# Attention stage of a decoder trunk: head weighting moved between the two halves of the key projection, softmax work put ahead of the query and key splits

## The chip, the cores and the metric

The kernel runs on one core of one Trainium2 chip. The metric is the device time of one execution in microseconds (us). A core has TensorE (PE in the rows, with its weight loads as PEld), VectorE (DVE), ScalarE (ACT), GpSimd (POOL) and SyncE (SP), which work side by side and wait for each other by semaphores. Each engine takes its own instructions in order, so an instruction that waits holds back all that stands behind it on its engine.

## What is computed

A two-layer decoder trunk on 256 tokens of width 1024, in float32: a short-convolution mixer and a convolutional feed-forward layer, then a shared key/value projection, attention with 8 heads of width 128, and a second feed-forward layer. With 256 tokens there is one block of keys, so the attention is causal softmax attention with a linear distance bias. Cut to what the change touches:

```python
k, v = jnp.split(rmsnorm(x, kv_norm) @ w_kv, 2, axis=-1)
q = (rmsnorm(x, norm_mix[1]) @ b_w_q[0]).reshape(b, s, N_HEADS, HEAD_DIM)
# for each head h and each 128 queries
s_own = einsum("bhqd,bhsd->bhqs", q_c, k_own) * scale - slopes * dist
p = softmax(where(dist >= 0, s_own, -inf))
o = einsum("bhqs,bhsd->bhqd", p, v_own)
x = x + o @ b_w_o[0]
```

## The kernel before

**Precision.** Every float32 product is made as three matmuls of rounded parts: each operand is split into a high part (a rounding copy on ScalarE) and a low part (the rest, a subtraction on VectorE). High times high, high times low and low times high are added up in PSUM. So every weight and every intermediate passes ScalarE and then VectorE before TensorE may use it.

**Weights** come in slots of 128x2048. SyncE loads them into a ring of six raw buffers; `hi(s)` (L354) rounds slot s on ScalarE, `lo(s)` (L616) subtracts on VectorE and counts `w_lo_ready`. Three places hold split slots, and a fourth (`SPARE`) a slot that is split ahead of its turn: `hi_ahead(2)` and `lo_ahead(2)` do that for the second slot of the last feed-forward layer.

**Attention** goes by pairs of heads, p = 0 to 3. Slots K and Q of pair p+1 are projected while pair p passes its softmax, so that TensorE's loop (L1207, p = 0 to 2) holds, in order: the projection of K for pair p+1 in two halves of one head each (`project(sK, 0, hA, e)`, into PSUM `pair0`), the weighting of V by the probabilities of pair p-1 (`weigh`), the scores of pair p (`scores`), the projection of Q for pair p+1 (`wide_slot`, into `pair1`), and the transposes of the probabilities of pair p (`transpose_probs`). Scores, transposed probabilities and weighted values of a head lie in one PSUM bank (`head_bank`). The banks of `acc[0]` and `acc[1]` take turns by pair, and the last pair has `pair0`.

**Helpers on the other two engines**, each once on ScalarE and once on VectorE: `kq_copy(i)` (L482) and `kq_whole(i)` (L789) add the two PSUM parts of projection i, `kq(i)` (L486, L794) splits the sum into `kq_hi` and `kq_lo`. `row_max` (L806 to L812, VectorE) adds the distance bias and finds the row maximum, `exp` (L475, ScalarE) follows, then `normal_probs` (L817, L820, VectorE). `heads_probs` (L581, L891) splits the transposed probabilities into `pt_hi` and `pt_lo`, for which `weigh` waits. `heads_mixed` (L586, L897) splits the weighted values into `mix_hi` and `mix_lo`, which the output projection reads.

**Order** is written out by hand on every engine. In the loop ScalarE and VectorE handle K of pair p+1 to its end (`kq_copy`/`kq_whole`, then `kq`), then the weighted values of pair p-1, then the softmax of pair p, then weight slot KQ0+2p+5, then Q of pair p+1, the transposed probabilities of pair p, and weight slot KQ0+2p+6.

**The tail** (L1229 to L1246): four slots of output weights, O0 to O0+3. `out_rows_of(i, t)` adds slot i for the tokens of half t into `acc[t]`. Before, the half t = 1 of O0 goes first, then the scores of heads 6 and 7, then the weighting of heads 4 and 5, then the half t = 1 of O0+1, and after that both halves t = 0.

Of the kernel before, what the change touches and what calls it, by code (L numbers as in the profile page):

```python
# [35 lines left out]
def build(nc, x, norm_mix, norm_ffn, ffn_w_up, ffn_conv, ffn_conv_b, ffn_w_down,  # L36
# [3 lines left out]
    KD = D // P  # L40
# [62 lines left out]
    with ExitStack() as ctx:  # L103
# [145 lines left out]

        def head_bank(h):  # L250

            return pair[0][:, h % 2, :] if h >= NH - 2 else acc[h // 2 % 2][h % 2][:]

        block = ctx.enter_context(nc.Block())

# [97 lines left out]
        def _(act):  # L353
            def hi(s, turn=None):  # L354

                act.wait_ge(landed[s % RAW], after(16 * (s // RAW + 1), turn, 16 * (TURN // RAW)))
                if s >= SPLIT:
                    act.wait_ge(slot_done, after(before(s) + 1, turn, TURN))
                act.activation(split_slot(s)[0], raw[:, s % RAW, :], ACT.Copy).then_inc(w_hi_ready, 2 if s + 1 in AHEAD else 1)  # L359

            def hi_ahead(o):
                s = AHEAD[o]
                act.wait_ge(landed[s % RAW], 16 * (s // RAW + 1))
                if o == 2:
                    act.wait_ge(slot_done, O0)
                act.activation(split_slot(s)[0], raw[:, s % RAW, :], ACT.Copy).then_inc(ahead_hi, 1)
# [104 lines left out]
            def exp(h):  # L471
                e = h % 2
                act.wait_ge(nbias_ready, h + 1)
                for t, cols in ((0, slice(0, 128)), (1, slice(128, 384))):
                    act.activation(logits[:, e, cols], logits[:, e, cols], ACT.Exp, bias=nbias[:, e, t:t + 1],  # L475
                                   scale=SCALE, accum_out=psums[:, e, t:t + 1]).then_inc(exp_ready, 1)

            def kq_copy(i):
                act.wait_ge(slot_done, KQ0 + i + 1)
                if i >= 2:  # L480
                    act.wait_ge(kq_lo_ready, i - 1)
                act.activation(whole[:, i % 2], cross[i % 2], ACT.Copy).then_inc(kq_cross, 1)  # L482

            def kq(i):
                act.wait_ge(kq_sum, i + 1)
                act.activation(kq_hi[:, i // 2 % 2, i % 2, :].rearrange("p (e n) -> p e n", e=2), whole[:, i % 2],  # L486
                               ACT.Copy).then_inc(kq_hi_ready, 1)
# [95 lines left out]
            def heads_mixed(p):  # L583
                for e in range(2):
                    act.wait_ge(heads_out, 2 * p + e + 1)
                    act.activation(mix_hi[:, 2 * p + e, :], head_bank(2 * p + e)[:, 0:256], ACT.Copy).then_inc(mix_hi_ready, 1)  # L586

            for p in range(NH // 2 - 1):
                kq_copy(2 * p + 2)
                kq(2 * p + 2)  # L590
                if p:
                    heads_mixed(p - 1)
                exp(2 * p)
                exp(2 * p + 1)
                hi(KQ0 + 2 * p + 5)
                kq_copy(2 * p + 3)
                kq(2 * p + 3)
                heads_probs(p)
                if p < NH // 2 - 2:
                    hi(KQ0 + 2 * p + 6)  # L600
            hi(O0 + 2)
            heads_mixed(NH // 2 - 2)
            exp(NH - 2)
            exp(NH - 1)
            hi_ahead(2)
            heads_probs(NH // 2 - 1)
            hi(O0 + 3)
            heads_mixed(NH // 2 - 1)
# [6 lines left out]
        def _(dve):  # L615
            def lo(s, turn=None):  # L616

                dve.wait_ge(w_hi_ready, after(s + 1, turn, TURN))
                whi, wlo = split_slot(s)
                dve.tensor_tensor(wlo, raw[:, s % RAW, :], whi.bitcast(F32),  # L620
                                  ALU.subtract).then_inc(w_lo_ready, 2 if s + 1 in AHEAD else 1)
# [165 lines left out]
            def kq_whole(i):  # L787
                dve.wait_ge(kq_cross, i + 1)
                dve.tensor_tensor(whole[:, i % 2], whole[:, i % 2], main[i % 2], ALU.add).then_inc(kq_sum, 1)  # L789

            def kq(i):
                dve.wait_ge(kq_hi_ready, i + 1)
                parts = [k[:, i // 2 % 2, i % 2, :].rearrange("p (e n) -> p e n", e=2) for k in (kq_hi, kq_lo)]
                dve.tensor_tensor(parts[1], whole[:, i % 2], parts[0].bitcast(F32), ALU.subtract).then_inc(kq_lo_ready, 1)  # L794
# [7 lines left out]
            def row_max(h):  # L802

                e = h % 2
                dve.wait_ge(scores_ready, h + 1)
                dve.scalar_tensor_tensor(out=logits[:, e, :], in0=dist[:], scalar=SLOPE[h] / SCALE, in1=head_bank(h)[:, 0:384],  # L806
                                         op0=ALU.mult, op1=ALU.add).then_inc(logits_ready, 1)
                dve.wait_ge(logits_ready, h + 1)
                dve.reduce_max(mx[:, e, 0:1], logits[:, e, 0:128], AX_X).then_inc(max_ready, 1)
                dve.reduce_max(mx[:, e, 1:2], logits[:, e, 128:384], AX_X).then_inc(max_ready, 1)  # L810
                dve.wait_ge(max_ready, 2 * h + 2)
                dve.tensor_scalar(nbias[:, e, :], mx[:, e, :], -SCALE, None, ALU.mult).then_inc(nbias_ready, 1)  # L812
# [81 lines left out]
            def heads_mixed(p):  # L894
                for e in range(2):
                    dve.wait_ge(mix_hi_ready, KD // 2 + 2 * p + e + 1)
                    dve.tensor_tensor(mix_lo[:, 2 * p + e, :], head_bank(2 * p + e)[:, 0:256],  # L897
                                      mix_hi[:, 2 * p + e, :].bitcast(F32), ALU.subtract).then_inc(mix_lo_ready, 1)

            for p in range(NH // 2 - 1):  # L900
                kq_whole(2 * p + 2)
                kq(2 * p + 2)
                if p:
                    heads_mixed(p - 1)
                row_max(2 * p)
                row_max(2 * p + 1)
                normal_probs(2 * p)
                normal_probs(2 * p + 1)
                lo(KQ0 + 2 * p + 5)
                kq_whole(2 * p + 3)  # L910
                kq(2 * p + 3)
                heads_probs(p)
                if p < NH // 2 - 2:
                    lo(KQ0 + 2 * p + 6)
            row_max(NH - 2)
            row_max(NH - 1)
            heads_mixed(NH // 2 - 2)
            normal_probs(NH - 2)
            normal_probs(NH - 1)
            lo(O0 + 2)  # L920
            lo_ahead(2)
            heads_probs(NH // 2 - 1)
            lo(O0 + 3)
            heads_mixed(NH // 2 - 1)
# [6 lines left out]
        def _(pe):  # L931
# [247 lines left out]
            def scores(h):  # L1179
                e, par = h % 2, h // 2 % 2  # L1180
                dst = head_bank(h)
                pe.wait_ge(kq_lo_ready, 2 * (h // 2) + 2)
                if NH - 4 <= h < NH - 2:
                    pe.wait_ge(mix_lo_ready, KD // 2 + h - 3)
                K = (kq_hi[:, par, 0, 256 * e:256 * e + 256], kq_lo[:, par, 0, 256 * e:256 * e + 256])
                Q = (kq_hi[:, par, 1, 256 * e:256 * e + 256], kq_lo[:, par, 1, 256 * e:256 * e + 256])
                split_matmul(dst[:, 0:P], ([q[:, 0:P] for q in Q], [k[:, 0:P] for k in K]), True, True)
                split_matmul(dst[:, P:3 * P], ([q[:, P:2 * P] for q in Q], K), True, True).then_inc(scores_ready, 1)
# [18 lines left out]
            for p in range(NH // 2 - 1):  # L1207
                sK, sQ = KQ0 + 2 * p + 2, KQ0 + 2 * p + 3
                wait_slot(sK)
                pe.wait_ge(kq_sum, 2 * p + 1)  # L1210
                for e in range(2):
                    last = project(sK, 0, hA, e)
                last.then_inc(slot_done, 1)
                if p:
                    weigh(2 * p - 2)
                    weigh(2 * p - 1)
                scores(2 * p)
                scores(2 * p + 1)
                pe.wait_ge(kq_sum, 2 * p + 2)
                wide_slot(sQ, 1, hB)  # L1220
                transpose_probs(2 * p)
                transpose_probs(2 * p + 1)
# [5 lines left out]

            p = NH // 2 - 1  # L1229
            wait_slot(O0)  # L1230
            pe.wait_ge(mix_lo_ready, KD // 2 + 4)
            out_rows_of(0, 1)
            scores(2 * p)
            scores(2 * p + 1)
            weigh(2 * p - 2)
            weigh(2 * p - 1)
            wait_slot(O0 + 1)
            out_rows_of(1, 1)
            pe.wait_ge(mix_lo_ready, KD // 2 + 6)
            out_rows_of(0, 0).then_inc(slot_done, 1)  # L1240
            transpose_probs(2 * p)
            transpose_probs(2 * p + 1)
            out_rows_of(1, 0).then_inc(slot_done, 1)
            weigh(2 * p)
            weigh(2 * p + 1)
            finish(O0 + 2, mix_pair(2), (mix_lo_ready, KD // 2 + 6), mix_pair(3), (mix_lo_ready, KD // 2 + 8), 4)  # L1246
# [22 lines left out]
```

## Time and profile before

| | us |
|---|---|
| runs | 599.85, 598.63, 599.07 |
| median | 599.07 |
| profiled execution, its own time | 599.85 |
| its span, first to last instruction | 598.0 |
| TensorE busy in the span | 583.9 (98%) |
| VectorE busy | 421.2 (70%) |
| ScalarE busy | 314.4 (53%) |
| mean granted TensorE clock | 0.996 |

The time of an execution is its span and some 1.9 us around it. The loop and tail of the attention stage lie between about 325 and 402 us of the span.

### The profile page before, as it was taken

What the parts mean: (1) busy time and instruction counts of PE and PEld (TensorE: products, weight loads), DVE (VectorE), ACT (ScalarE), POOL (GpSimd) and SP (SyncE); (2) the same over time, 40 slices, a digit from 0 to 9 for tenths busy, and PEclk for the clock granted to TensorE, in tenths of its full rate; (3) what the DMA queues carried; (4) which work ended last, traced back from release to release, by engine and by line L of the source; (5) the groups of instructions that cost most, each with busy time, mean ns of one, the idle gap of its engine ahead of it and who ended that gap; (6) DMA issues with size and microseconds to landing.
All of it is one profiled execution on the core that took longest, in us unless ns stands there. A gap on an engine that the chain in (4) does not pass through costs nothing.

```text
span 598.0 us, 8163 instructions
## 1 busy us (share of the span) xinstructions
PE 583.9 (98%) x3119; PEld 498.6 (83%) x3119; DVE 421.2 (70%) x508; ACT 314.4 (53%) x380; POOL 10.1 (2%) x22
## 2 busy tenths in 40 slices
PE   8999999999999999999999989899999999999995
PEld 6988888888888888888878878788888888888884
DVE  4688876678666666668786778787686666666764
ACT  5543563566545445546445655645674545544541
POOL 2000000000000000000100000000000000000000
PEclk9999999999999999999999999899999999999999
DMA  8995658354566556555565344263556655654001
GB/s 282 344 296 200 216 184 276 122 200 162 192 211 211 179 173 210 192 166 196 181 210 178 144 140 142 71 219 122 204 193 212 209 168 186 210 180 170 0 0 71
DMA packets 80911, 107.99 MB, mean 181 GB/s; under 512 B 1833, under 2 KB 71665, under 8 KB 80882
## 3 DMA queue, kind: packets, MB, share of 16 engines
q1 hardware_dynamic: 80160, 104.97, 53.1%
q10 hardware_dynamic: 722, 2.63, 1.3%
q8 instruction: 19, 0.31, 0.2%
q14 instruction: 10, 0.08, 0.0%
HBM read 106.54 MB, written 1.05 MB: 180 GB/s over the span
## 4 chain that ended last, share of the span: by engine, by line
PE 90%; DVE 5%; ACT 3%; issue 1%; POOL 0%; ACTq 0%; DVEq 0%; POOLq 0%
PE pair L951 33%; PE pair L952 17%; PE acc L993 8%; PE acc L995 8%; PE acc L997 8%; PE pair L935 3%; PE pair L937 3%; PE pair L936 3%; DVE wgt L620 2%; ACT wgt L359 2%; PE pair L1007 2%; PE acc L937 1%; PE acc L936 1%; PE acc L935 1%; PE acc L1116 1%
## 5 line engine op out<-in xcount | busy, mean ns | idle before, releaser
L951 PE MATMUL pair<-hA,wgt 128*128 128x512 f32 x864 | 304.7, 397 | 0.0
L620 DVE TENSOR_TENSOR wgt<-raw,wgt 128x2048 fp32r<-128x2048 f32 x94 | 214.9, 2291 | 62.3 <-ACT wgt L359 62.3
L952 PE MATMUL pair<-hA,wgt 128*128 128x256 f32 x864 | 241.4, 279 | 0.0
L951 PEld LDWEIGHTS pair<-hA,wgt 128*128 128x128 f32 x864 | 162.2, 188 | 38.7
L359 ACT ACTIVATE wgt<-raw 128x2048 fp32r<-128x2048 f32 x94 | 179.4, 1912 | 26.3 <-PE acc L997 22.8
L952 PEld LDWEIGHTS pair<-hA,wgt 128*128 128x128 f32 x864 | 162.8, 188 | 0.6
L993 PE MATMUL acc<-wgt,kq_hi 128*128 128x512 f32 x160 | 49.8, 392 | 0.0
L995 PE MATMUL acc<-wgt,kq_hi 128*128 128x512 f32 x160 | 49.7, 392 | 0.0
L997 PE MATMUL acc<-wgt,kq_lo 128*128 128x512 f32 x160 | 49.3, 389 | 0.0
L426 ACT ACTIVATE scratch<-scratch 128x512 f32<-128x512 f32 x22 | 13.9, 632 | 59.7 <-DVE scratch L698 59.7
L440 ACT ACTIVATE scratch<-pair 128x512 f32<-128x512 f32 x20 | 11.9, 595 | 59.9 <-PE pair L952 59.9
L719 DVE TENSOR_TENSOR scratch<-scratch,pair 128x512 f32<-128x512 f32 x20 | 13.7, 686 | 32.6 <-ACT scratch L440 32.6
L995 PEld LDWEIGHTS acc<-wgt,kq_hi 128*128 128x128 f32 x160 | 30.0, 188 | 6.8
L935 PE MATMUL pair<-wgt,hA 128*128 128x512 f32 (+1 forms) x96 | 34.7, 362 | 1.0 <-DVE v_lo L799 1.0
L997 PEld LDWEIGHTS acc<-wgt,kq_lo 128*128 128x128 f32 x160 | 30.0, 188 | 6.7
L937 PE MATMUL pair<-wgt,hA 128*128 128x512 f32 (+1 forms) x96 | 34.1, 355 | 0.0
L936 PE MATMUL pair<-wgt,hA 128*128 128x512 f32 (+1 forms) x96 | 34.0, 354 | 0.0
L993 PEld LDWEIGHTS acc<-wgt,kq_hi 128*128 128x128 f32 x160 | 28.8, 188 | 5.7
L698 DVE SCALAR_TENSOR_TENSOR scratch<-scratch,f_par 128x255 f32<-128x255 f32 (+1 forms) x80 | 33.2, 477 | 0.0
L723 DVE TENSOR_TENSOR scratch<-scratch,pair 128x512 f32<-128x512 f32 x20 | 13.8, 688 | 23.7 <-ACT scratch L447 23.7
L377 ACT ACTIVATE acc<-xs 128x512 f32<-128x512 f32 x20 | 12.0, 602 | 27.3 <-DVE xs L631 24.0
L418 ACT ACTIVATE scratch<-scratch,f_par 128x256 f32<-128x256 f32 x40 | 21.6, 590 | 1.5 <-DVE scratch L719 1.5
(143 smaller groups left out, 610.0 us busy)
## 6 DMA issues: line engine op xcount, KB each, us to landing
raw<-in_ffn_w_up SPq DMA_DIRECT2D x44, 1024.0 KB, 5.1
raw<-in_ffn_w_down SPq DMA_DIRECT2D x22, 1024.0 KB, 4.8
raw<-in_a_w_in SPq DMA_DIRECT2D x11, 1024.0 KB, 11.5
raw<-in_w_kv SPq DMA_DIRECT2D x8, 1024.0 KB, 5.2
raw<-in_a_w_out SPq DMA_DIRECT2D x4, 1024.0 KB, 4.9
raw<-in_b_w_q SPq DMA_DIRECT2D x4, 1024.0 KB, 5.6
raw<-in_b_w_o SPq DMA_DIRECT2D x4, 1024.0 KB, 5.3
raw<-in_a_w_in SPq DMA_DIRECT2D x2, 512.0 KB, 7.1
```

Of the source, the lines that this page charges most:

```text
L359: act.activation(split_slot(s)[0], raw[:, s % RAW, :], ACT.Copy).then_inc(w_hi_ready, 2 if s + 1 in AHEAD else 1)
L418: ins = act.activation(g[:, e, :], gate[:, e, :], ACT.Identity, bias=f_par[:, l, bass.ds(f + TAPS * FT, 1)], scale=f_par[:, l, bass.ds(f + ...
L620: dve.tensor_tensor(wlo, raw[:, s % RAW, :], whi.bitcast(F32), ALU.subtract).then_inc(w_lo_ready, 2 if s + 1 in AHEAD else 1)
L698: dve.scalar_tensor_tensor(out=dst, in0=gate[:, e, 0:S - back], scalar=f_par[:, l, bass.ds(f + (TAPS - 1 - back) * FT, 1)], in1=dst, op0=A ...
L935: pe.matmul(dst, sh, mh, start=first, stop=False)
L936: pe.matmul(dst, sh, ml, start=False, stop=False)
L937: return pe.matmul(dst, sl, mh, start=False, stop=last)
L951: pe.matmul(dst.rearrange("p (a n) -> p a n", a=2), whi[:, w], hid[:, :, k, :], start=k == 0, stop=False)
L952: last = pe.matmul(dst[:, 0:S], wlo[:, w], hid[:, 0, k, :], start=False, stop=k == KD - 1)
L993: pe.matmul(acc[t][h][:], ah, wh[h], start=first, stop=False)
L995: pe.matmul(acc[t][h][:], ah, wl[h], start=False, stop=False)
L997: last = pe.matmul(acc[t][h][:], al, wh[h], start=False, stop=False)
```

## The change

**PSUM banks.** `head_bank` gives `acc[1]` to all heads below 6; the pairs no longer take turns. In return every `scores(h)` with h of 2 or more waits for `mix_lo` of head h-2, the last reader of what lay in the bank.

**Loop on TensorE.** The two `weigh` calls move from behind both halves of the K projection to a place between them.

**Loop on ScalarE and VectorE.** `heads_mixed(p-1)` moves ahead of `kq_copy`/`kq_whole(2p+2)`, and `kq(2p+2)` moves from directly behind it to behind the softmax and weight slot KQ0+2p+5.

**Tail.** The half t = 0 of O0 and O0+1 goes first (it reads `mix_lo` of fewer heads and writes the free `acc[0]`), `weigh` of heads 4 and 5 stands ahead of the scores of heads 6 and 7, and `hi_ahead(2)`/`lo_ahead(2)` stand ahead of `heads_mixed(2)`, with slot O0+2 split later in exchange. On VectorE `heads_mixed(2)` comes ahead of the row maxima of heads 6 and 7.

The diff of the loop and the tail on TensorE and of the loop on VectorE (ScalarE's is the same in kind):

```diff
-            return pair[0][:, h % 2, :] if h >= NH - 2 else acc[h // 2 % 2][h % 2][:]
+            return pair[0][:, h % 2, :] if h >= NH - 2 else acc[1][h % 2][:]
...
             for p in range(NH // 2 - 1):
-                kq_whole(2 * p + 2)
-                kq(2 * p + 2)
                 if p:
                     heads_mixed(p - 1)
+                kq_whole(2 * p + 2)
                 row_max(2 * p)
                 row_max(2 * p + 1)
                 normal_probs(2 * p)
                 normal_probs(2 * p + 1)
                 lo(KQ0 + 2 * p + 5)
+                kq(2 * p + 2)
                 kq_whole(2 * p + 3)
                 kq(2 * p + 3)
                 heads_probs(p)
...
+            lo_ahead(2)
+            heads_mixed(NH // 2 - 2)
             row_max(NH - 2)
             row_max(NH - 1)
-            heads_mixed(NH // 2 - 2)
             normal_probs(NH - 2)
             normal_probs(NH - 1)
             lo(O0 + 2)
-            lo_ahead(2)
...
-                if NH - 4 <= h < NH - 2:
-                    pe.wait_ge(mix_lo_ready, KD // 2 + h - 3)
+                if h >= 2:
+                    pe.wait_ge(mix_lo_ready, KD // 2 + h - 1)
...
-                for e in range(2):
-                    last = project(sK, 0, hA, e)
-                last.then_inc(slot_done, 1)
+                project(sK, 0, hA, 0)
                 if p:
                     weigh(2 * p - 2)
                     weigh(2 * p - 1)
+                project(sK, 0, hA, 1).then_inc(slot_done, 1)
...
-            pe.wait_ge(mix_lo_ready, KD // 2 + 4)
-            out_rows_of(0, 1)
+            pe.wait_ge(mix_lo_ready, KD // 2 + 2)
+            out_rows_of(0, 0)
+            weigh(2 * p - 2)
+            weigh(2 * p - 1)
             scores(2 * p)
             scores(2 * p + 1)
-            weigh(2 * p - 2)
-            weigh(2 * p - 1)
             wait_slot(O0 + 1)
-            out_rows_of(1, 1)
+            pe.wait_ge(mix_lo_ready, KD // 2 + 4)
+            out_rows_of(1, 0)
             pe.wait_ge(mix_lo_ready, KD // 2 + 6)
-            out_rows_of(0, 0).then_inc(slot_done, 1)
+            out_rows_of(0, 1).then_inc(slot_done, 1)
             transpose_probs(2 * p)
             transpose_probs(2 * p + 1)
-            out_rows_of(1, 0).then_inc(slot_done, 1)
+            out_rows_of(1, 1).then_inc(slot_done, 1)
```

What stands where, first on VectorE in the loop at p = 1, before. `wgt<-raw` is a weight slot's `lo`, `scratch<-scratch,pair` is `kq_whole`, `kq_lo` is `kq`, `pt_lo` is `heads_probs`, `mix_lo` is `heads_mixed`, and `scratch<-dist,acc` opens `row_max`:

```order
L620 TENSOR_TENSOR wgt<-raw,wgt 128x2048 [waits w_hi_ready]
L789 TENSOR_TENSOR scratch<-scratch,pair1 128x512 [waits kq_cross]
L794 TENSOR_TENSOR kq_lo<-scratch,kq_hi 128x512 [waits kq_hi_ready]
L891 TENSOR_TENSOR pt_lo<-acc00,pt_hi 128x384 [waits pt_hi_ready]
L891 TENSOR_TENSOR pt_lo<-acc01,pt_hi 128x384 [waits pt_hi_ready]
L620 TENSOR_TENSOR wgt<-raw,wgt 128x2048 [waits w_hi_ready]
L789 TENSOR_TENSOR scratch<-scratch,pair0 128x512 [waits kq_cross]
L794 TENSOR_TENSOR kq_lo<-scratch,kq_hi 128x512 [waits kq_hi_ready]
L897 TENSOR_TENSOR mix_lo<-acc00,mix_hi 128x256 [waits mix_hi_ready]
L897 TENSOR_TENSOR mix_lo<-acc01,mix_hi 128x256 [waits mix_hi_ready]
L806 SCALAR_TENSOR_TENSOR scratch<-dist,acc10 128x384 [waits scores_ready]
```

The same stretch of VectorE in the changed kernel:

```order
L620 TENSOR_TENSOR wgt<-raw,wgt 128x2048 [waits w_hi_ready]
L794 TENSOR_TENSOR kq_lo<-scratch,kq_hi 128x512 [waits kq_hi_ready]
L789 TENSOR_TENSOR scratch<-scratch,pair1 128x512 [waits kq_cross]
L794 TENSOR_TENSOR kq_lo<-scratch,kq_hi 128x512 [waits kq_hi_ready]
L891 TENSOR_TENSOR pt_lo<-acc10,pt_hi 128x384 [waits pt_hi_ready]
L891 TENSOR_TENSOR pt_lo<-acc11,pt_hi 128x384 [waits pt_hi_ready]
L620 TENSOR_TENSOR wgt<-raw,wgt 128x2048 [waits w_hi_ready]
L897 TENSOR_TENSOR mix_lo<-acc10,mix_hi 128x256 [waits mix_hi_ready]
L897 TENSOR_TENSOR mix_lo<-acc11,mix_hi 128x256 [waits mix_hi_ready]
L789 TENSOR_TENSOR scratch<-scratch,pair0 128x512 [waits kq_cross]
L806 SCALAR_TENSOR_TENSOR scratch<-dist,acc10 128x384 [waits scores_ready]
```

The K split has left the place between `kq_whole` and the row maximum, and stands between the weight slot and Q's `kq_whole`, so ahead of `pt_lo`.

TensorE in the tail, around heads 4 to 7, in the changed kernel (`acc10<-pt_hi,v_hi` is `weigh`, `pair0<-kq_hi` is `scores`, `wgt,mix_hi` is an output slot):

```order
L997 MATMUL acc01<-wgt,mix_lo 128x512
L935 MATMUL acc10<-pt_hi,v_hi 128x256 [waits pt_lo_ready]
...
L937 MATMUL acc11<-pt_hi,v_lo 128x128
L935 MATMUL pair0<-kq_hi 128x128 [waits mix_lo_ready,kq_lo_ready]
...
L937 MATMUL pair0<-kq_hi,kq_lo 128x256
L993 MATMUL acc00<-wgt,mix_hi 128x512 [waits mix_lo_ready,w_lo_ready]
```

Before, the scores stood ahead of the weighting here and waited for `kq_lo_ready` alone; now they stand behind it and wait for `mix_lo` of the values that it makes.

## Rows read from the trace of the kernel before

**Rows 1.** The page: the chain that ended last, by engine.

```profile
PE 90%; DVE 5%; ACT 3%; issue 1%; POOL 0%; ACTq 0%; DVEq 0%; POOLq 0%
```

**Rows 2.** Waits between 325 and 402 us: waiter, releaser, us in total, times, longest.

```profile
ACT kq_hi L486 <- DVE scratch L789: 13.9, 7, 2.5
DVE wgt L620 <- ACT wgt L359: 8.4, 9, 1.1
...
PE acc L1194 <- DVE scratch L820: 3.2, 4, 1.0
...
PE pair L935 <- DVE kq_lo L794: 2.0, 1, 2.0
```

**Rows 3.** Timeline of PE in the loop: start us, us, instruction, idle before and releaser.

```profile
333.75 0.22 PE L935 MATMUL acc<-kq_hi 128*128 128x128 f32 x1
...
341.43 0.47 PE L951 MATMUL pair<-hA,wgt 128*128 128x512 f32 x1
...
344.29 0.39 PE L951 MATMUL pair<-hA,wgt 128*128 128x512 f32 x1
...
347.06 0.28 PE L935 MATMUL acc<-pt_hi,v_hi 128*128 128x256 f32 x1
...
348.38 0.28 PE L935 MATMUL acc<-kq_hi 128*128 128x128 f32 x1
...
349.82 0.40 PE L951 MATMUL pair<-wgt 128*128 128x512 f32 x1
...
356.54 0.55 PE L1194 MATMUL acc<-ident,scratch 128*128 128x128 f32 x3 [1.01 <-DVE scratch L820]
...
358.00 0.47 PE L951 MATMUL pair<-hA,wgt 128*128 128x512 f32 x1
```

**Rows 4.** Timeline of PE in the tail.

```profile
374.56 0.70 PE L993 MATMUL acc<-wgt,mix_hi 128*128 128x512 f32 x2
...
379.58 0.33 PE L935 MATMUL pair<-kq_hi 128*128 128x128 f32 x1 [2.04 <-DVE kq_lo L794]
...
381.06 0.33 PE L935 MATMUL acc<-pt_hi,v_hi 128*128 128x256 f32 x1
...
383.43 1.16 PE L993 MATMUL acc<-wgt,mix_hi 128*128 128x512 f32 x2
```

**Rows 5.** Timeline of DVE in the loop and the tail.

```profile
334.57 0.69 DVE L789 TENSOR_TENSOR scratch<-scratch,pair 128x512 f32<-128x512 f32 x1
335.96 0.69 DVE L794 TENSOR_TENSOR kq_lo<-scratch,kq_hi 128x512 fp32r<-128x512 f32 x1 [0.70 <-ACT kq_hi L486]
336.57 0.55 DVE L806 SCALAR_TENSOR_TENSOR scratch<-dist,acc 128x384 f32<-128x384 f32 x1
...
342.12 2.29 DVE L620 TENSOR_TENSOR wgt<-raw,wgt 128x2048 fp32r<-128x2048 f32 x1 [1.05 <-ACT wgt L359]
344.33 0.68 DVE L789 TENSOR_TENSOR scratch<-scratch,pair 128x512 f32<-128x512 f32 x1
...
346.32 1.01 DVE L891 TENSOR_TENSOR pt_lo<-acc,pt_hi 128x384 fp32r<-128x384 f32 x2
...
384.08 0.42 DVE L897 TENSOR_TENSOR mix_lo<-acc,mix_hi 128x256 fp32r<-128x256 f32 x1 [0.46 <-ACT mix_hi L586]
```

**Rows 6.** Timeline of ACT in the loop and the tail.

```profile
333.94 0.60 ACT L482 ACTIVATE scratch<-pair 128x512 f32<-128x512 f32 x1 [1.75 <-PE pair L952]
...
340.20 1.90 ACT L359 ACTIVATE wgt<-raw 128x2048 fp32r<-128x2048 f32 x1
...
346.33 1.91 ACT L359 ACTIVATE wgt<-raw 128x2048 fp32r<-128x2048 f32 x1
```

**Rows 7.** Stretches: bounds, length, each engine's busy us (count), granted clock, DMA.

```profile
372.00:374.00 2.00, 0.64 (x4) 0.31 (x3) 1.49 (x8) 1.68 (x7) 0.00 (x0) 1.00 0.00 0
...
382.00:383.00 1.00, 1.00 (x7) 1.00 (x6) 0.97 (x3) 0.38 (x1) 0.00 (x0) 0.50 0.03 9
...
385.00:386.00 1.00, 1.00 (x6) 0.83 (x5) 0.83 (x4) 1.00 (x5) 0.00 (x0) 1.00 0.00 0
```

More of the change, by code:

```diff
@@ L588, in _ @@
             for p in range(NH // 2 - 1):
-                kq_copy(2 * p + 2)
-                kq(2 * p + 2)
                 if p:
                     heads_mixed(p - 1)
+                kq_copy(2 * p + 2)
                 exp(2 * p)
@@ L600, in _ @@
                     hi(KQ0 + 2 * p + 6)
-            hi(O0 + 2)
+            hi_ahead(2)
             heads_mixed(NH // 2 - 2)
@@ L604, in _ @@
             exp(NH - 1)
-            hi_ahead(2)
+            hi(O0 + 2)
             heads_probs(NH // 2 - 1)
@@ L900, in _ @@
             for p in range(NH // 2 - 1):
-                kq_whole(2 * p + 2)
-                kq(2 * p + 2)
                 if p:
                     heads_mixed(p - 1)
+                kq_whole(2 * p + 2)
                 row_max(2 * p)
@@ L909, in _ @@
                 lo(KQ0 + 2 * p + 5)
+                kq(2 * p + 2)
                 kq_whole(2 * p + 3)
```

## The prediction

> **What bounds the kernel now.** I read the chain that ended last first: 90% of it is TensorE [rows 1], so time can only be won or lost where TensorE stands idle or runs slowly. The list of waits then says where that is. In the attention stage TensorE waits four times for the probabilities, 3.2 us in all, and once 2.0 us for `kq_lo` of the last pair [rows 2]. The order behind 402 us is the same in both kernels, and with the chain on TensorE I take it that what such a wait gains or loses moves the end by as much.
>
> The timelines show why it waits. One turn of the loop takes 16.57 us (341.43 to 358.00), of which TensorE's own work is less: K projection 5.63 (341.43 to 347.06), `weigh` 1.32, `scores` 1.44 (to 349.82), Q projection as long as K without its restart, 5.56, and two sets of transposes, 0.75; together 14.7. So 1.87 us of each turn are a stall, seen in front of the transposes [rows 3]. The other side is a ring of ScalarE and VectorE: VectorE waits for each weight slot's high part (8.4 us in nine waits) and ScalarE for each `kq_whole` (13.9 us in seven) [rows 2]. The two alternate and set the turn; TensorE trails.
>
> In the tail TensorE starts the last scores at 379.58 after 2.04 us idle, and then runs slowly: the two `weigh` take 2.37 us (381.06 to 383.43) in place of 1.32, and the first pair of output matmuls 1.16 in place of 0.70 [rows 3, 4]. The granted clock there is 0.50, which is 1.2 GHz, and it is 1.00 (2.4 GHz) again from 385 on. Before it fell, TensorE had been idle for 2.04 us. The shorter stalls in the loop (1.01 us and one more just behind it, with TensorE busy for 0.64 of 2 us) left it at 1.00 [rows 7]. I count the slow stretch at 1.05 + 0.46, about 1.5 us.
>
> **The change part by part.** I carry three dates through the loop, on the clock of the trace of before; until 334 us nothing differs.
>
> *K's split leaves the place ahead of the row maximum.* `kq_whole(2)` starts at 334.57 and now the row maximum follows it after 0.61 us (the spacing of such an operation, 335.96 to 336.57), at 335.18 and not 336.57: 1.39 us earlier [rows 5]. The scores are there by then (they start at 333.75 and take 1.44, head by head) [rows 3]. This carries on through the exponentials to `hi(KQ0+5)`, 340.20 before and 338.81 now [rows 6], and its `lo`, 342.12 before and 340.73 now [rows 5].
>
> *It comes back ahead of Q's.* Behind `lo` stands now `kq_lo` of K, 0.61 us, and only then Q's `kq_whole`, on which `pt_lo` hangs. Of 1.39 us won 0.78 is left for `pt_lo`: it starts at 345.54 and not 346.32, and its first head is ready 0.55 later, at 346.09 [rows 5].
>
> *`weigh` moves ahead of the second half of K.* This is the term on which all hangs. Before, TensorE came to `weigh` at 347.06, after 5.63 us of K, and `pt_lo` was just there. Now it comes after half of K, at 344.29, and finds `pt_lo` missing until 346.14: a stall of 1.85 us [rows 3]. The stall in front of the transposes goes, since the softmax is done 1.4 us earlier and TensorE comes later. One stall takes the place of the other.
>
> *The ring is now closed through TensorE.* `kq_copy` of K needs both halves of K, and the second now stands behind `weigh`, so also behind `pt_lo`. One turn of the new ring, each step from rows: `weigh` 1.32 and second half 2.77 (344.29 to 347.06) [rows 3]; from K's end to ScalarE's copy 0.20 (333.75 to 333.94) [rows 3, 6]; copy 0.63 (to 334.57); `kq_whole` 0.61; row maximum to `hi` 3.63 (336.57 to 340.20); `hi` to `lo` 1.92; `lo` 2.21 (342.12 to 344.33); `kq_lo` 0.61; `kq_whole` to `pt_lo` 1.99 (344.33 to 346.32); `pt_lo` of the first head 0.55 and 0.05 to TensorE [rows 5, 6]. The sum is 16.49 us, against 16.57 before. The loop wins 0.1 us a turn and no more. `weigh` of heads 4 and 5 starts at 346.14 + 2 x 16.49 = 379.12.
>
> *The new wait of the scores for `mix_lo`, in the loop.* It waits behind the whole second half of K. `mix_lo` of both heads follows `lo(KQ0+6)`, which starts at 345.54 + 0.01 + 1.92 = 347.47 and frees VectorE at 349.68; the first head is ready 0.42 later at 350.10. TensorE wants it at 346.14 + 1.32 + 2.77 = 350.23. I take nothing for it. Its cover is 0.13 us; behind the scores stand the Q projection and the transposes, so what is late here is paid in full.
>
> *The tail.* Behind `pt_hi` of heads 4 and 5 ScalarE does `hi_ahead(2)` first: `pt_lo` starts at 378.52, `hi_ahead` at 378.53 as `hi` did beside it before (346.32 and 346.33) [rows 5, 6], `lo_ahead` 1.92 later at 380.45, then 2.21 of VectorE to 382.66, and only then `mix_lo`, 0.42 for head 4 [rows 5], with 0.05 at 383.13. The scores of heads 6 and 7 wait for that. TensorE has ended `weigh` at 379.12 + 1.32 = 380.44 and stands for 2.7 us. Scores end at 383.13 + 1.44 = 384.57. Before, the same point (slot O0+1 begins) was at 383.43, or at 382.38 without the slow clock [rows 4]. The change **loses 2.2 us** here. Behind it no new wait: by the same steps the last probabilities are ready at about 388.5 and wanted at 390.1, `pt_lo` of head 6 at 392.3 and wanted at 393.6, `mix_lo` of head 7 at 396.4 and wanted at 397.7, so 1.2 us of cover at the least. Using one bank pair for all heads, the other order of the output halves, and the later `hi`/`lo` of O0+2 cost nothing beyond these waits.
>
> *The clock.* Before had one long stall (2.04 us) and one slow stretch (1.5 us). The changed kernel has five: 1.85 at p = 1, 16.49 - 14.7 = 1.8 at p = 2, and in the tail 1.8, then 1.3 us of work, then 2.7. Bounds for the two in the loop: nothing each, as after the stalls of 1.0 us, or 1.5 each, as after that of 2.04. They are nearer to the second, but a little shorter; I take one of the two. For the tail pair I take one slow stretch as before, between 1.0 (partly under the 2.7 us wait) and 3 (it reaches into the output slots).
>
> By the Trainium skill ("TensorE: Matmul & The Clock Gate", section "Why this matters for your kernels") the clock is lost in idle gaps longer than any single one here. The trace of before disagrees, since its 2.04 us sufficed; by that rule the sum would lack every slow stretch and be 600.5, the second case below.
>
> **Sum.** Profiled execution 599.85 + 2.2 + 1.5 = 603.6. The median lies 0.8 below the profiled execution, perhaps for want of the slow stretch, so the forecast is **602.8**, 0.6% above 599.07.
>
> **The rivals.**
>
> *The clock stays up.* All of the above holds but no stall brings the clock down: 599.85 - 1.5 + 2.2 = 600.5. For it: stalls of 1.85 and less are not 2.04. Against it: two of them, 1.8 and 2.7, lie within 6 us. 0.12.
>
> *Trade one for one.* The loop is even as computed and the tail's wait is short, because `mix_lo` comes early, where `lo_ahead` is done by the time `weigh` ends. That needs 2.2 us less than the rows give: 599.1. 0.06.
>
> *The stalls go (faster).* If `pt_lo` were ready when TensorE comes to `weigh`, at 344.3, the ring would be short, and TensorE's 14.7 us would be the turn: 2 x 1.87 won in the loop, 2.0 for `kq_lo` of the last pair and 1.5 of slow clock, 7.3 in all, 591.8. It decides at 1.8 us: so much earlier must `pt_lo` be. Against it stand four rows in series (`lo` 2.21, `kq_lo` 0.61, `kq_whole` to `pt_lo` 1.99). 0.05.
>
> *The scores' wait bites in the loop too.* If heads' splitting is over 0.13 us later than I count, each turn pays the rest, and a slow stretch may follow at both loop stalls: with two more slow stretches and 0.5 us a turn, 599.1 + 2.2 + 3 + 1 = 605.3 and more. 0.05.
>
> **How the numbers follow.** Forecast 0.72, its own range from 601.3 (no slow stretch in the loop) to 604.6 (two). The range to hold eight in ten starts at the second case, 600.5, and ends at 605.2. A measurement of this kernel can tell about 0.2% (1.2 us) from no change. Slower by over that: 0.72 + 0.09 + 0.05 = 0.86; the second case lies just at this bound, and gives 0.03 to "same", which with the trade is 0.09; faster is 0.05.
>
> **What would show it.** In the changed kernel's list of waits `weigh` (PE L935) must wait for `pt_lo` L891 three times, for 1.8 us each, the scores in the tail once for `mix_lo` L897 for 2.7, and the transposes hardly at all; a turn of the loop must be 16.5 us; stretches at clock 0.50 must follow the stalls. It is wrong if the transposes still wait, if a turn is near 14.7, or if the scores at p = 1 wait for `mix_lo`.

## The result and the profile after

The changed kernel is slower: 605.35 us median (603.85 to 606.12) against 599.46 us for the kernel before beside it, a ratio of 1.0096 with a 95% interval of 1.0076 to 1.0115. In a second comparison it took 604.19 us (603.67 to 606.1) against 600.1, a ratio of 1.0077 (1.0061 to 1.0093). The forecast of 602.8 had the direction right and the size too small: +3.7 us was forecast, and +5.9 and +4.1 were measured. The first median, of four runs, lies 0.15 us above the range. The record of the first comparison has fifteen executions of the changed kernel, from 603.57 to 606.82 us with a median of 605.17, so the true middle lies close to the range's upper end.

The waits of TensorE's instructions between 325 and 408 us of the changed kernel (waiter, releaser, us in total, times, longest), to be held against [rows 2]:

```profile
PE acc L935 <- DVE pt_lo L891: 5.5, 3, 1.9
...
PE pair L935 <- DVE mix_lo L897: 2.5, 1, 2.5
```

The 3.2 us in front of the transposes (L1194) and the 2.0 us for `kq_lo` are gone. In their place `weigh` (acc L935) waits three times for `pt_lo`, and the scores of heads 6 and 7 (pair L935) once for `mix_lo`. Here are the places in time (start us, us, instruction, idle before it and its releaser), beside [rows 3, 4]:

```profile
333.14 0.22 PE L935 MATMUL acc<-kq_hi 128*128 128x128 f32 x1
...
345.54 0.39 PE L935 MATMUL acc<-pt_hi,v_hi 128*128 128x256 f32 x1 [1.82 <-DVE pt_lo L891]
...
351.38 0.22 PE L935 MATMUL acc<-kq_hi 128*128 128x128 f32 x1
...
363.79 0.39 PE L935 MATMUL acc<-pt_hi,v_hi 128*128 128x256 f32 x1 [1.83 <-DVE pt_lo L891]
...
368.05 0.22 PE L935 MATMUL acc<-kq_hi 128*128 128x128 f32 x1
...
380.45 0.39 PE L935 MATMUL acc<-pt_hi,v_hi 128*128 128x256 f32 x1 [1.87 <-DVE pt_lo L891]
...
384.57 0.44 PE L935 MATMUL pair<-kq_hi 128*128 128x128 f32 x1 [2.53 <-DVE mix_lo L897]
...
387.27 1.05 PE L993 MATMUL acc<-wgt,mix_hi 128*128 128x512 f32 x2
...
394.32 0.82 PE L1194 MATMUL pair<-ident,scratch 128*128 128x128 f32 x6
```

The second turn, from `weigh` to `weigh`, is 16.66 us (363.79 to 380.45). The first is 18.25 us (345.54 to 363.79), and the clock tells why. These are stretches of the changed kernel (bounds, length, each engine's busy us, granted clock, DMA), beside [rows 7]:

```profile
346.00:348.00 2.00, 2.00 (x12) 2.00 (x11) 1.12 (x1) 1.31 (x3) 0.00 (x0) 0.56 0.31 127
348.00:350.00 2.00, 2.00 (x9) 1.66 (x9) 1.84 (x3) 0.20 (x1) 0.00 (x0) 0.58 0.00 0
...
364.00:366.00 2.00, 2.00 (x17) 1.91 (x17) 1.06 (x2) 1.76 (x3) 0.00 (x0) 1.00 0.52 178
382.00:384.00 2.00, 0.04 (x1) 0.00 (x0) 2.00 (x1) 0.42 (x2) 0.00 (x0) 0.95 0.00 0
384.00:386.00 2.00, 1.43 (x7) 1.46 (x8) 0.76 (x3) 0.00 (x0) 0.00 (x0) 0.50 0.00 0
...
388.00:390.00 2.00, 2.00 (x6) 1.52 (x6) 1.49 (x8) 1.68 (x9) 0.00 (x0) 0.50 0.00 0
390.00:392.00 2.00, 2.00 (x9) 1.62 (x8) 0.91 (x4) 1.76 (x1) 0.00 (x0) 0.84 0.03 8
```

A mean clock of 0.56 over 2 us says that TensorE spent 1.76 us of them at 0.50, which is 1.2 GHz. So it ran slowly for 3.4 us between 346 and 350, behind the first stall. It did so again for 6.8 us, from just ahead of 384 until inside 390 to 392, behind the stalls of 1.87 and 2.53 us. In the kernel before, the one slow stretch lasted 3.4 us (381.2 to 384.6). Behind the stall at p = 2, which was as long as that at p = 1, the clock stayed at 1.00.

What the low clock cost can be read off the start times. The measure is the same piece of work at full clock: for `weigh` to the scores that of p = 2 above, and for the tail these rows of the changed kernel with its stalls filled (first experiment below):

```profile
384.07 0.30 PE L935 MATMUL pair<-kq_hi 128*128 128x128 f32 x1 [1.35 <-DVE mix_lo L897]
...
385.53 0.63 PE L993 MATMUL acc<-wgt,mix_hi 128*128 128x512 f32 x2
...
390.99 0.82 PE L1194 MATMUL pair<-ident,scratch 128*128 128x128 f32 x6
```

From `weigh` to the scores TensorE took 5.84 us at p = 1 (345.54 to 351.38) and 4.26 at p = 2 (363.79 to 368.05): 1.6 us. The last scores took 2.70 us (384.57 to 387.27) in place of 1.46: 1.2 us. The two half slots of output weights after them took 7.05 us (387.27 to 394.32) in place of 5.46: 1.6 us. Together the slow clock cost 4.4 us in this execution. In the profiled execution of before it cost 1.6: 1.05 on `weigh`, and 0.6 on the half slots, which took 6.08 (383.43 to the transposes at 389.51) and 5.5 in the kernel before with its stall filled.

The mean clock is 1.00 from 0 to 325 us and from 402 to 584 us in each of the ten profiles, so a slow clock in another stage plays no part.

### The profile page after: what moved, and what is told of

Same layout as the page of the kernel before. It is cut to its first block, busy times and chain, and to the rows that moved or that the text cites. A ratio compares the mean times of both kernels' runs of the same rounds, so it can differ in the third digit from the quotient of the medians.

```text
span 602.9 us, 8168 instructions
## 1 busy us (share of the span) xinstructions
PE 585.9 (97%) x3119; PEld 501.0 (83%) x3119; DVE 421.4 (70%) x508; ACT 314.7 (52%) x380; POOL 10.1 (2%) x22
## 3 DMA queue, kind: packets, MB, share of 16 engines
HBM read 106.54 MB, written 1.05 MB: 178 GB/s over the span
## 4 chain that ended last, share of the span: by engine, by line
PE 91%; DVE 5%; ACT 3%; issue 1%; POOL 0%; DVEq 0%; ACTq 0%; POOLq 0%
PE pair L951 34%; PE pair L952 17%; PE acc L993 8%; PE acc L995 8%; PE acc L997 8%; PE pair L935 3%; PE pair L937 3%; PE pair L936 3%; PE pair L1007 2%; DVE wgt L620 2%; PE acc L935 1%; PE acc L937 1%; PE acc L936 1%; ACT wgt L359 1%; PE acc L1116 1%
## 5 line engine op out<-in xcount | busy, mean ns | idle before, releaser
L935 PE MATMUL pair<-wgt,hA 128*128 128x512 f32 (+1 forms) x96 | 34.7, 362 | 1.0 <-DVE v_lo L799 1.0
```

The costliest lines, as they stand in the source:

```text
L935: pe.matmul(dst, sh, mh, start=first, stop=False)
```

## The experiments

Theory A says that the loss is the stalls' (about 2.2 us) and that all the rest is the clock that falls behind them. Its rivals: the rest is something else (B), one part of the change gives back what it wins (C), or the place of `weigh` alone costs the time and the single bank pair nothing (D).

### All stalls filled

```diff
                 project(sK, 0, hA, 0)
                 if p:
+                    fill(acc[0][1][:, 0:P], 4)
                     weigh(2 * p - 2)
...
             out_rows_of(0, 0)
+            pe.wait_ge(kq_sum, NH - 1)
+            fill(pair[0][:, 0, 0:P], 4)
             weigh(2 * p - 2)
             weigh(2 * p - 1)
+            fill(pair[0][:, 0, 0:P], 5)
             scores(2 * p)
```

`fill(bank, n)` issues n matmuls of the identity into a bank that is free then; the trace shows two matmul records for each call.

> The changed kernel, with matmuls of the identity (results unused) put into its stalls: 4 calls ahead of the weighting at p = 1 and 2, 4 ahead of that in the tail, 5 ahead of the scores of heads 6 and 7. They keep TensorE busy while it waits and should not move a wait's end. Theory A (the waits cost 2.2 us, all the rest of the loss is the clock that falls after them): no stretch below clock 1.00 between 325 and 402 us, and 599.5 - 1.0 (the clock's share in the kernel before) + 2.2 = 600.7, between 600.0 and 601.4. Theory B (the rest is something else, late work on the other engines or a transfer): about as the changed kernel, 604.5 to 605.5.

Measured: 601.36 us median, and twelve runs lie between 601.0 and 601.73. TensorE's waits between 325 and 402 us:

```profile
PE acc L935 <- DVE pt_lo L891: 2.9, 3, 1.0
PE pair L935 <- DVE mix_lo L897: 1.4, 1, 1.4
```

The clock in the same kernel:

```profile
340.00:355.00 15.00, 14.07 (x95) 12.67 (x94) 11.33 (x20) 7.53 (x14) 0.00 (x0) 1.00 0.41 141
...
380.00:390.00 10.00, 8.65 (x54) 7.73 (x55) 7.22 (x18) 5.12 (x12) 0.00 (x0) 1.00 0.13 45
```

Nothing useful was added and no wait ends sooner: the first `weigh` starts 12.40 us behind the first scores, as in the changed kernel (333.14 to 345.54). The fillers only halve the idle time that is seen (1.82 to 0.93 us at p = 1). The clock stays at 1.00 and 2.8 us (against 604.19) to 4.0 us (against 605.35) are gone, from comparisons that ran apart. That is 0.7 us above theory A's figure and at the upper end of its range. Theory B's 604.5 to 605.5 was missed by 3 us and more, and B falls.

### The stall of the kernel before filled

```diff
             out_rows_of(0, 1)
+            pe.wait_ge(kq_sum, NH - 1)
+            fill(pair[0][:, 0, 0:P], 4)
             scores(2 * p)
```

> The kernel before, with 4 such calls of identity matmuls (results unused) in its one long stall, ahead of the scores of heads 6 and 7. Theory A: the slow stretch behind 381 us goes, 598.4 (597.9 to 598.9), and the runs lie closer together. Theory B: no change, 599.5.

Measured: 598.62 us (597.72 to 599.1) against 599.62 (598.25 to 601.25); the ratio is 0.9981 (0.9971 to 0.9991). The clock's share in the kernel before is 1.0 us on the median. The 32 unfilled runs beside it say the same without any filler. Ten of them have a mean granted clock of 0.997 or 0.998 and took 598.6 us on average, as the filled kernel did. The other 22 have 0.993 to 0.996 and took 600.1. So the slow stretch costs 1.5 us and seems to fall in about two runs of three. With both kernels filled the change costs 601.36 - 598.62 = 2.7 us: the stalls, nearly clean of the clock.

### The tail filled alone

The edit of the first experiment without the `fill` in the loop.

> The changed kernel with the identity matmuls (results unused) in the two stalls of the tail alone; those of the loop stay empty. Theory A, with the sizes of the changed kernel's profile (slow clock 2.7 us in the tail, 1.7 in the loop): 605.3 - 2.7 = 602.6 (602.0 to 603.3), 1.3 above the kernel with all stalls filled. If the clock of the loop costs nothing: 601.4. If that of the tail costs nothing: 605.3.

Measured: 602.86 us (601.67 to 604.01), within theory A's range. That is 1.3 below the changed kernel that ran beside it (the tail's clock) and 2.5 below that of the first comparison. It is 1.5 above the kernel with all stalls filled (the loop's clock), which ran apart; with each taken against its own kernel before it is 1.0 (2.76 - 1.74). So the medians show that both places cost something, but not how much each to better than 1 us. In the profile the clock fell at both loop stalls, for 3.4 us each:

```profile
348.00:350.00 2.00, 2.00 (x7) 1.66 (x7) 2.00 (x2) 0.21 (x1) 0.00 (x0) 0.50 0.00 0
...
366.00:368.00 2.00, 2.00 (x10) 1.81 (x9) 2.00 (x2) 0.53 (x2) 0.00 (x0) 0.50 0.00 0
```

### The changed kernel again

> The changed kernel once more, beside these. All theories: 605.3 (604.7 to 605.9).

Measured: 604.19 us (603.67 to 606.1), 0.5 us below the range that was expected. In its profile the stall at p = 1 was the same 1.83 us, but only the tail ran slowly:

```profile
346.68 0.39 PE L935 MATMUL acc<-pt_hi,v_hi 128*128 128x256 f32 x1 [1.83 <-DVE pt_lo L891]
```

```profile
346.00:348.00 2.00, 1.32 (x12) 1.32 (x12) 1.09 (x3) 2.00 (x3) 0.00 (x0) 1.00 0.95 391
348.00:350.00 2.00, 2.00 (x14) 1.76 (x14) 1.97 (x1) 0.65 (x2) 0.00 (x0) 1.00 0.00 0
...
384.00:386.00 2.00, 1.82 (x9) 1.85 (x9) 0.53 (x3) 0.00 (x0) 0.00 (x0) 0.50 0.00 0
386.00:388.00 2.00, 2.00 (x8) 1.81 (x8) 1.90 (x7) 0.72 (x3) 0.00 (x0) 0.50 0.00 0
```

So the same stall in the same kernel brings the clock down in one execution and not in another. In the tail it was down for 6.8 us again, 1.5 of them while TensorE stood still:

```profile
384.18 0.45 PE L935 MATMUL pair<-kq_hi 128*128 128x128 f32 x1 [2.52 <-DVE mix_lo L897]
...
386.88 1.05 PE L993 MATMUL acc<-wgt,mix_hi 128*128 128x512 f32 x2
...
393.60 0.82 PE L1194 MATMUL pair<-ident,scratch 128*128 128x128 f32 x6
```

The scores took 2.70 us and the half slots 6.72, which puts the cost at 1.2 + 1.3 = 2.5 us.

### The wait of the last scores taken away

Heads 6 and 7 lie in `pair0`, and the bank that the wait guards is not theirs.

```diff
-                if h >= 2:
+                if 2 <= h < NH - 2:
                     pe.wait_ge(mix_lo_ready, KD // 2 + h - 1)
```

> The changed kernel; the scores of heads 6 and 7 no longer wait for mix_lo, since they lie in pair0 and not in the bank that heads 4 and 5 use. By the rows the stall of 2.5 us goes, and the weighting of head 6 comes to wait 0.7 us for pt_lo: 1.8 us less. Theory A: the second stall in the tail no longer follows close on the first, so one slow stretch less: 605.3 - 1.8 - 1.5 = 602.0 (601.3 to 602.7). Theory B (stalls alone): 603.5.

Measured: 601.62 us (600.37 to 603.19), 3.7 below the changed kernel of the first comparison and 2.6 below that of the second. The 2.53 us stall is gone, and `weigh` waits as before, 5.6 us in three. But in the profiled execution the slow stretch in the tail did not get shorter, though only one stall of 1.89 us was left ahead of it:

```profile
378.00:380.00 2.00, 0.25 (x1) 0.25 (x2) 1.47 (x3) 2.00 (x4) 0.00 (x0) 0.96 0.95 330
380.00:382.00 2.00, 2.00 (x11) 2.00 (x11) 1.06 (x2) 1.45 (x2) 0.00 (x0) 0.50 0.54 183
...
386.00:388.00 2.00, 2.00 (x9) 1.59 (x8) 1.49 (x8) 1.68 (x7) 0.00 (x0) 0.83 0.00 0
```

The slow stretch lasted 6.8 us here too, so that its double length comes from two stalls close together is not borne out by this one profile. The time does not decide between the theories either. Theory A's 602.0 and B's 603.5 were reckoned from 605.3; reckoned from 604.19 they are 600.9 and 602.4, and the measured time lies between. The wait of 0.7 us for `pt_lo` of head 6 that was expected in its place did not show, since the slow clock brought TensorE there late (394.67, with `pt_lo` begun at 392.32).

### The split of K moved, and nothing else

```diff
                 kq_whole(2 * p + 2)
-                kq(2 * p + 2)
...
                 lo(KQ0 + 2 * p + 5)
+                kq(2 * p + 2)
                 kq_whole(2 * p + 3)
```

(and the same on ScalarE).

> The kernel before, with one part of the change alone: the split of K (kq(2p+2)) behind the softmax and the weight slot, on ScalarE and VectorE; TensorE's order and the banks as before. Theory A (the ring of ScalarE and VectorE sets the turn, and this part shortens it by 0.8 us; the loss is all from moving weigh ahead of pt_lo and from the tail): stalls in the loop fall from 1.9 us a turn to 0.1 and 0.6 to 0.8, the wait for kq_lo in the tail grows from 2.0 to 2.8: 2.3 us less, 597.2 (596.6 to 598.4 with the clock). Theory C (the split put ahead of Q's kq_whole gives back what it won): 599.3 to 599.7.

Measured: 597.47 us (595.79 to 598.7), a ratio of 0.996 (0.9947 to 0.9973), as theory A expected (597.2). This part of the change alone makes the kernel faster. All of TensorE's waits between 325 and 402 us:

```profile
PE pair L935 <- DVE kq_lo L794: 2.6, 1, 2.6
PE acc L1194 <- DVE scratch L820: 0.5, 1, 0.5
PE acc L935 <- DVE pt_lo L891: 0.3, 1, 0.3
```

The 3.2 us in front of the transposes [rows 2] have become 0.5, and C falls. Behind the 2.64 us of idleness in the tail the clock stayed at 1.00 in this profile, which is of one of the four quickest runs (595.8 to 596.3 us, mean clock 0.997 or 0.998). The other eight took 597.1 to 598.7 at 0.995 or 0.996, so there it presumably fell; they were not profiled. The rows:

```profile
376.00:378.00 2.00, 0.69 (x6) 0.69 (x7) 1.44 (x3) 2.00 (x4) 0.00 (x0) 1.00 0.98 329
378.00:380.00 2.00, 2.00 (x20) 2.00 (x19) 1.82 (x6) 1.47 (x2) 0.00 (x0) 1.00 0.54 182
```

### `weigh` back behind K

```diff
                 project(sK, 0, hA, 0)
+                project(sK, 0, hA, 1).then_inc(slot_done, 1)
                 if p:
                     weigh(2 * p - 2)
                     weigh(2 * p - 1)
-                project(sK, 0, hA, 1).then_inc(slot_done, 1)
```

> The changed kernel with weigh back behind both halves of K in the loop; its one bank pair, the wait of every scores for mix_lo, the order of the other engines and the tail stay. Theory A: weigh finds pt_lo ready, but the scores behind it must now wait for mix_lo, which hangs on weigh itself and on the weight slot: stalls of 2.0 us at p = 1, 1.4 at p = 2, 1.4 and 2.7 in the tail, 1.3 us less than changed, and the shorter stall at p = 2 may spare a slow stretch: 603.7 (602.6 to 604.6). Theory D (weigh's place alone costs the time, the bank pair nothing): about 599.5 + 1 for the tail, 600.5.

Measured: 603.34 us (602.04 to 604.37), as theory A expected (603.7), and D falls (600.5). In the loop the stalls moved from `weigh` to the scores, which now wait for what `weigh` has only just made: 1.8 us at p = 1 and 0.3 at p = 2, where 2.0 and 1.4 were expected. The tail keeps both of its stalls:

```profile
PE pair L935 <- DVE mix_lo L897: 2.5, 1, 2.5
PE acc L935 <- DVE mix_lo L897: 2.1, 2, 1.8
PE acc L935 <- DVE pt_lo L891: 1.6, 1, 1.6
```

So one bank pair for all heads is itself a part of the cost. With it `weigh` must stand early, and then `pt_lo` is late; or `weigh` stands late, and then `mix_lo` is.

### Another order from the same parts

The kernel before with its two bank pairs, its instructions and its waits, in another order on all three engines. On TensorE the loop and the start of the tail read:

```diff
+            key_half(0, 0); scores(0); key_half(0, 1); scores(1)
+            query_half(0, 0); transpose_probs(0); query_half(0, 1)
+            key_half(1, 0); key_half(1, 1); scores(2); transpose_probs(1); scores(3)
+            query_half(1, 0); query_half(1, 1); weigh(0); transpose_probs(2)
+            key_half(2, 0); weigh(1); key_half(2, 1); transpose_probs(3)
+            scores(4); weigh(2); scores(5)
+            query_half(2, 0); weigh(3); query_half(2, 1); transpose_probs(4)
...
```

On ScalarE and VectorE a weight slot is split one place earlier, the sum of a projection stands ahead of its split, and the softmax goes head by head.

> The kernel before (its banks, its waits) with another order written out for the loop and the tail on all three engines: weight slots are split one place earlier, K's and Q's copies stand ahead of the splits, head by head instead of pair by pair, transposes and weighting half a projection later. By the durations of the rows no stall of over 0.1 us is left between 334 and 397 us. Theory A: 6.4 us of stalls and the clock's 1.0 us go: 592.1 (591.6 to 593.2). Theory E (the contention of more closely packed engines, or a transfer, takes part of it): 594 to 597.

Measured: 592.85 us (592.17 to 592.98) against 600.1, a ratio of 0.9879 (0.9863 to 0.9895). The list of waits has no row left for TensorE between 325 and 402 us. It is busy and at full clock:

```profile
340.00:355.00 15.00, 15.00 (x93) 13.27 (x91) 13.27 (x24) 7.77 (x13) 0.00 (x0) 1.00 0.61 211
355.00:370.00 15.00, 15.00 (x102) 13.70 (x101) 13.15 (x27) 11.05 (x25) 0.00 (x0) 1.00 0.44 141
370.00:380.00 10.00, 10.00 (x62) 8.78 (x62) 8.66 (x23) 5.43 (x11) 0.00 (x0) 1.00 0.31 105
```

It beats both kernels, by what theory A gave (592.1, up to 593.2); theory E, that more closely packed engines or a transfer take part of it (594 to 597), falls. The same 3119 matmuls are issued in all three kernels, so what was won is idle time and slow clock, and TensorE has neither left in this stage.

## Why the prediction was right in its mechanism and short in its size

**Where TensorE stands idle, as forecast.** The loop's ring closes through `pt_lo`. The stalls at `weigh` were put at 1.85, 1.8 and 1.8 us and measured at 1.82, 1.83 and 1.87. The turn was put at 16.49 us and was 16.66 where the clock did not fall. The new wait of the scores was seen in the tail alone, 2.7 forecast and 2.53 measured, and the 0.13 us of cover in the loop held. The transposes' waits and that for `kq_lo` went. The prediction speaks of five long stalls and lists four; four there were.

**The stalls' cost in all**, 2.2 us forecast, measured 2.7 as the difference of the two filled kernels. The profiles give the same, each with its own slow clock and its own start of the stage taken off (us):

| profile | its time | first scores at | slow clock cost | what is left |
|---|---|---|---|---|
| before | 599.85 | 333.75 | 1.6 | 264.5 |
| before, stall filled | 599.00 | 334.50 | 0 | 264.5 |
| changed | 604.68 | 333.14 | 4.4 | 267.1 |
| changed again | 603.95 | 334.27 | 2.5 | 267.2 |
| changed, tail filled | 604.00 | 333.75 | 3.1 | 267.1 |
| changed, all filled | 601.30 | 334.13 | 0 | 267.2 |

Of the 0.5 us that the forecast lacked, 0.3 is in the two turns. `weigh` at p = 2 took 1.43 us and not 1.32, because TensorE's first matmul after a stall took 0.22 us to the next (345.54 to 345.76) where it took 0.12 without one (347.06 to 347.18 in the kernel before). The stage began at 333.14 to 334.50 us in these profiles, a spread found with both kernels, whose cause is not shown.

**The clock was the term mis-sized.** The forecast gave it 1.5 us more than in the kernel before: one stall in the loop with a slow stretch of 1.5, and one stretch in the tail as before. The loop's part was right in this profile, 1.6. The step that failed is the tail's, "I take one slow stretch as before". In both profiles of the changed kernel the tail's stretch lasted 6.8 us, and in that of before 3.4. It reached through the scores into the output slots and cost 2.8 and 2.5 us, not the 1.5 counted (1.6 by the start times above). I had named that bound (3 us) and chosen the lower value. On medians the clock costs the changed kernel 4.0 us (605.35 - 601.36) or 2.8 (604.19 - 601.36), and the one before 1.0 (599.62 - 598.62). The change added 1.8 to 3.0 us by the clock, not 1.5. How the medians divide that between loop and tail is not settled, as said at the kernel with the tail filled.

**The median against the profiled execution** is a second step that failed. The forecast took 0.8 us off because the profiled execution of before was above the median of its three runs, "perhaps for want of the slow stretch". But 599.85 was no high run: the medians beside the experiments are 599.62 (32 runs) and 600.1 (11 runs). And a run of the kernel before can lack its only slow stretch, while the changed kernel has four stalls of which any can bring one. It was profiled at 604.68 and has a median of 605.35, so nothing was to be taken off. Of the 2.55 us between 602.8 and 605.35, 1.1 is the profiled execution (604.68 against 603.6: 1.3 for the clock and 0.5 for the stalls, less 0.6 because its stage began earlier), and 1.5 is this step.

**The rivals.** "The clock stays up" was to give 600.5; with the stalls filled that case was made and gives 601.36. "The scores' wait bites in the loop too" was to give 605.3 and more, which is the time measured, but its mechanism is absent: in the loop the scores waited only where `weigh` was put back. The other two did not come about.

**The Trainium skill** ("TensorE: Matmul & The Clock Gate", section "Why this matters for your kernels") was read as clearing stalls as short as these. The traces of the changed kernel disagree as that of before did, since the clock fell behind 1.82 us.

**What stays open** is what decides whether a stall of 1.8 to 2.6 us brings the clock down, and for how long. The same stall did and did not, and the long stretch in the tail stood behind two stalls in three profiles and behind one of 1.89 us in a fourth. Open too is how the loss divides between the shared bank pair and the new order of the tail on ScalarE and VectorE, which no run has by itself.

## What to carry to other kernels

When work is moved on the bound engine, redo the date of what it waits for: here moving `weigh` up by half a projection only moved a wait of 1.9 us from one place to another, and closed the ring of the other two engines through TensorE. Taking operations off the ring (K's split behind the softmax) was worth 2.1 us by itself, but the rest of the change cost more than that. Sharing one bank pair ties the scores to the weighting, and in the tail alone taking that wait away won 2.6 to 3.7 us (comparisons that ran apart), though it guarded a bank that those scores do not use. A stall of about 2 us on TensorE is to be priced with the clock behind it: in these profiles 1.6 us on top where it fell for 3.4 us and 2.5 to 2.8 where it fell for 6.8.

## What the runs showed of the hardware

- Slow stretches at 1.2 GHz followed stalls of 1.8 to 2.0 us, yet one of 2.64 us passed without any. Five of the nine in the ten profiles lasted 3.4 us and four lasted 6.8, the long ones all in the tails of kernels with `weigh` ahead of the last scores.
- How often the clock falls goes with the spread of the runs: 0.7 us over twelve runs with the stalls filled, against 3.3 us over the fifteen of the changed kernel. Within the kernel before, runs at a mean clock of 0.997 or more took 1.5 us less than the others.
- A few matmuls of the identity in a stall kept the clock at 1.00 behind every stall so filled, in three profiles, though half the idle time stays. Their worth was 1.0 us for 4 calls in the kernel before.
